# Chunked modulation with k-wise latents, conv units joined into the query stage, and a new split of the first up units, in a one-core layer kernel on Trainium2

## The reference, cut to what matters

```python
mod_lat = silu(c) @ w_ada + b_ada              # 6 * 1024 values; the context takes silu(c_ctx)
h  = rmsnorm(x, norm1_g)   * (1 + sc1)  + sh1  # the first two of six groups
hc = rmsnorm(ctx, norm1_g) * (1 + csc1) + csh1
p  = h @ w_in                                  # [kv latent 256 | rope key 32 | q latent 384 | conv x, B, C 3 * 512 | gates]
pc = hc @ w_in[:, :288]
q  = rmsnorm(q latent, q_norm_g)  @ w_uq       # 8 heads of 64 + 32 rotary
k, v = rmsnorm(kv latent, kv_norm_g) @ w_ukv   # 768 keys
o  = softmax(q k^T / sqrt(96)) v               # heads 8, queries 512
y_conv = (b_gate * dwconv3(c_gate * x_in)) @ w_conv_out
x = x + g1 * ((sigmoid(ga) * (o @ w_attn_out) + sigmoid(gc) * y_conv) @ w_o)
x = x + g2 * (silu(gate) * val) @ w_down       # gate, val = split(dwconv3(modulated rmsnorm(x) @ w_up))
out = rmsnorm(x, final_g)
```

## Time and profile before

| | |
|---|---|
| median of three runs | 853.37 us (852.27 to 854.98) |
| the profiled execution | 852.57 us |
| its span, first to last instruction | 850.8 us |
| mean granted TensorE clock | 0.983 |
| PE busy | 808.2 us, 3900 matmuls |
| DVE, ACT, POOL busy | 471.8, 373.9, 376.0 us |
| moved by DMA | 97.79 MB |

### The profile page before, as it was taken

The page is one execution under the profiler, slowest core; times in us unless marked ns, Lnnn a source line. Parts: engine busy times, 40 slices in busy tenths (PEclk is TensorE's granted clock), DMA queues, the critical chain, the costliest instruction groups (busy, mean ns, idle before and its releaser), DMA issues.

```text
span 850.8 us, 11214 instructions
## 1 busy us (share of the span) xinstructions
PE 808.2 (95%) x3900; PEld 672.6 (79%) x3900; DVE 471.8 (55%) x600; ACT 373.9 (44%) x571; POOL 376.0 (44%) x191
## 2 busy tenths in 40 slices
PE   6779978999999999999999989999999999999996
PEld 4458856888888888888788978888888888888884
DVE  5854698788887467788413646555555555100005
ACT  7763365656565442232234644444444444211124
POOL 0086274345533455455455034444444444444434
PEclk9979999999999999999999989999999999999998
DMA  9822211111111488777355014333333332323312
GB/s 317 289 74 61 64 50 50 50 50 29 48 50 26 153 252 259 252 247 219 127 198 148 2 50 123 99 99 99 99 99 98 92 96 93 96 95 98 99 50 99
DMA packets 119134, 97.79 MB, mean 115 GB/s; under 512 B 13532, under 2 KB 100857, under 8 KB 119097
## 3 DMA queue, kind: packets, MB, share of 16 engines
q1 hardware_dynamic: 119065, 97.28, 37.1%
q10 hardware_dynamic: 32, 0.01, 0.0%
HBM read 95.17 MB, written 2.10 MB: 114 GB/s over the span
## 4 chain that ended last, share of the span: by engine, by line
PE 59%; issue 16%; POOL 9%; DVE 6%; DMA 4%; ACT 2%; SPq 2%; POOLq 0%; DVEq 0%; ACTq 0%
PE ps L374 16%; PE ps L375 15%; PE ps L376 15%; POOL wlo L318 8%; PE ps L1444 7%; PE ps L1426 3%; PE ps L1415 2%; DMA raw<-w_in_dram 2%; DMA raw<-w_o_dram 1%; POOL ht L525 1%; DMA xt<-ctx_dram 1%; DMA xt<-x_dram 1%; DVE wlo L318 1%; DVE work L1022 1%; SPq L425 1%
## 5 line engine op out<-in xcount | busy, mean ns | idle before, releaser
L318 POOL TENSOR_TENSOR wlo<-raw,whi 128x1024 fp32r<-128x1024 f32 (+4 forms) x126 | 287.8, 2292 | 423.8 <-ACT whi L310 401.6
L374 PE MATMUL ps<-hhi,whi 128*128 128x512 f32 (+1 forms) x560 | 214.7, 383 | 8.8 <-DVE hlo L962 5.3
L375 PE MATMUL ps<-hlo,whi 128*128 128x512 f32 (+1 forms) x560 | 213.5, 381 | 0.0
L376 PE MATMUL ps<-hhi,wlo 128*128 128x512 f32 (+1 forms) x560 | 213.2, 381 | 0.0
L310 ACT ACTIVATE whi<-raw 128x1024 fp32r<-128x1024 f32 (+3 forms) x127 | 123.3, 980 | 141.1 <-PE ps L376 77.8
L374 PEld LDWEIGHTS ps<-hhi,whi 128*128 128x128 f32 x560 | 106.8, 191 | 30.1 <-issue 6.4
L376 PEld LDWEIGHTS ps<-hhi,wlo 128*128 128x128 f32 x560 | 106.7, 191 | 20.0
L375 PEld LDWEIGHTS ps<-hlo,whi 128*128 128x128 f32 x560 | 106.8, 191 | 19.6 <-issue 0.2
L1208 DVE SCALAR_TENSOR_TENSOR work<-ps,prm,work 128x511 f32<-128x511 f32 x44 | 33.0, 750 | 82.0 <-ACT work L875 81.1
L1113 DVE SCALAR_TENSOR_TENSOR adacc<-ada,cvec,adacc 128x1024 f32<-128x1024 f32 x28 | 64.9, 2357 | 14.8 <-DMA ada<-w_ada_dram 14.8
L875 ACT ACTIVATE work<-ps,prm 128x512 f32<-128x512 f32 x44 | 34.2, 778 | 79.2 <-PE ps L376 79.2
(11 more groups left out here) (245 smaller groups left out, 1430.1 us busy)
## 6 DMA issues: line engine op xcount, KB each, us to landing
raw<-w_up_dram SPq DMA_DIRECT2D x88, 256.0 KB, 3.1
raw<-w_in_dram SPq DMA_DIRECT2D x66, 256.0 KB, 3.4
ada<-w_ada_dram SPq DMA_DIRECT2D x32, 512.0 KB, 6.1
raw<-w_down_dram SPq DMA_DIRECT2D x44, 256.0 KB, 2.7
adaraw<-w_ada_dram SPq DMA_DIRECT2D x32, 256.0 KB, 4.8
raw<-w_o_dram SPq DMA_DIRECT2D x16, 256.0 KB, 3.0
xt<-x_dram SPq DMA_DIRECT2D x4, 512.0 KB, 6.4
raw<-w_attn_out_dram SPq DMA_DIRECT2D x8, 256.0 KB, 2.9
```

Of the source, the lines that this page charges most:

```text
L318: ins = (engine or nc.gpsimd).tensor_tensor(out=l, in0=r, in1=h.bitcast(F32), op=ALU.subtract)
L374: pe.matmul(o, l[0], r[0], start=start, stop=False)
L375: pe.matmul(o, l[0], r[1], start=False, stop=False)
L376: return pe.matmul(o, l[1], r[0], start=False, stop=stop)
```

## The change

- The first two groups of the modulation (shift and scale) are made in four chunks of 256 columns. The first chunk's columns come directly by fp32 products of the unsplit weights with the two conditioning vectors as two moving columns (`first_mods`); the other chunks go through the split, are summed as rows (`mod_sums`) and turned into columns by a product with a 4 x 2 selection matrix `sel` that also adds the high and low parts (`mod_columns`).
- The latents are no longer computed unit by unit over all k, but k by k: one row block of `w_in` with the 640 latent columns at a time (`latents`, five banks at once), as soon as the tile k of `h` is there. The kv weights stay in SBUF (`lkhi`, `lklo`) and the context is computed with them later, beside the rotary key, whose unit is cut in two.
- DVE makes the modulated value (`stream_value`) that POOL made; POOL splits the latent weights (`latent_lo`).
- The two context token tiles come in later, into the buffers of the first tokens.
- The kv norm's root and reciprocal are taken on 6 columns (`k_rms`, `k_inv`) and spread by six products with the identity.
- The first two units of the first conv tile are computed between the query heads, in pieces of 8, the third unit in the first two groups of attention, in pieces of 12; the other three conv tiles follow in pieces of 8, 8, 8, 8, 8, 8, 6, 6, 6, 6 (`CONV_TURNS`). The conv steps of ACT and DVE move accordingly.
- The maximum of a group is written to a spare PSUM column of the scores' second bank (`top`) and no longer to SBUF.
- The second halves of the first four up units: two units together over all k, then one, then one, where there were four together.

```diff
 U_ADA = 0
-U_Q = U_ADA + 2 * DT
-U_KV = U_Q + QT
-U_KR = U_KV + KVT
-U_UQ = U_KR + 1
-U_V = U_UQ + HEADS // 2
+U_KR = U_ADA + 2 * DT - 4
+U_UQ = (U_KR + 2, U_KR + 3, U_KR + 5, U_KR + 6)
+U_CX0, U_CC0 = U_KR + 4, U_KR + 7
+U_V = U_KR + 8
...
-CONV_PIECES = ((0, 8), (0, 8), (0, 8), (1, 8), (1, 8), (1, 8), (2, 12), (2, 12))
+CONV_TURNS = ((0, 2, 0, 12), (0, 2, 12, 12)) + tuple(
+    (j, n, at, size) for j in range(1, CT) for n, size in ((0, 8), (1, 8), (2, 6)) for at in range(0, 3 * DT, size))
...
+            def ada_load(u):
+
+                if u < 0:
+                    at = 0
+                else:
+                    at = (u // 4 + 1) * CHUNK
+                    if u < SLOTS:
+                        sp.wait_ge(s("ada0_used"), u + 1)
+                    else:
+                        sp.wait_ge(w_lo, u - SLOTS + 1)
...
+            for c_ in range(CHUNKS):
+                latent_load(2 * c_)
+                latent_load(2 * c_ + 1)
+                if c_ in (1, 2):
+                    token_load(TT + c_ - 1)
+                if c_ + 1 < CHUNKS:
+                    for u in range(4 * c_, 4 * c_ + 4):
+                        ada_load(u)
...
+            for c_ in range(1, CHUNKS):
+                for u in range(4 * c_ - 4, 4 * c_):
+                    ada_hi(u)
+                mod_rows1(c_)
+                for k in (2 * c_, 2 * c_ + 1):
+                    latent_hi(k)
+                    stream_hi(k)
+                if c_ > 1:
+                    upper_copy(TT + c_ - 2)
+                if c_ < 3:
+                    token_rms(TT + c_ - 1)
...
+            def first_mods(n):
+
+                pe.wait_ge(ada_loaded[n], 32)
+                for i in range(2):
+                    for m in range(4):
+                        at = i * T + m * P
+                        last = pe.matmul(ps[:, 3, 2 * m:2 * m + 2], adaraw[:, n, at:at + P], cvec[:, 2 * n + i, :],
+                                         start=(n, i, m) == (0, 0, 0), stop=(n, i, m) == (3, 1, 3))
+                last.then_inc(s("ada0_used"), 1)
...
+            for c_ in range(CHUNKS):
+                latents(2 * c_, every)
+                if c_ == 0:
+                    latents(1, (0, 1, 2))
+                if c_ + 1 < CHUNKS:
+                    for u in range(4 * c_, 4 * c_ + 4):
+                        mod_sums(u)
+                    latents(2 * c_ + 1, (0,) if c_ else (3,))
+                    mod_columns(c_ + 1)
+                    latents(2 * c_ + 1, (1, 2, 3, 4) if c_ else (4,))
+                else:
+                    latents(2 * c_ + 1, every)
+                if c_ in (1, 2):
+                    token_columns(TT + c_ - 1)
...
+                if h == 1:
+                    pe.wait_ge(s("p_raw"), KVT)
+                    latent_sums()
+                if 1 <= h < 4:
+                    conv_piece(0, 0, 8 * (h - 1), 8)
+                if h == 2:
+                    spread_inverse()
+                if h >= 5:
+                    conv_piece(0, 1, 8 * (h - 5), 8)
...
-                nc.vector.reduce_max(neg_max(g), wide(2 * (turn(g) % 2)), AX.X, negate=True).then_inc(s("nmax"), 1)
+                top = ps[:, 2 * (turn(g) % 2) + 1, C:C + 1]
+                nc.vector.reduce_max(top, wide(2 * (turn(g) % 2)), AX.X, negate=True).then_inc(s("nmax"), 1)
...
-            for i in range(DT):
-                pe.wait_ge(s("h2_lo"), DT + i + 1)
-                for m in range(4):
-                    last = up_half(m, 1, i)
-                    if i == DT - 1:
-                        last.then_inc(w_used, 1)
+            for ms in ((0, 1), (2,), (3,)):
+                for i in range(DT):
+                    pe.wait_ge(s("h2_lo"), DT + i + 1)
+                    for m in ms:
+                        last = up_half(m, 1, i)
+                        if i == DT - 1:
+                            last.then_inc(w_used, 1)
```

More of the change, by code:

```diff
@@ L442, in _, with token_load @@
-            for m in range(4):
-                slot = (U_UQ + m) % SLOTS
-                view = raw[:, slot % RAW, 0:2 * QT * QK].rearrange("p (k h n) -> p k h n", k=QT, n=QK)
-                load(sp, U_UQ + m, slot, [(view[:, :, h, :], rows_of(w_uq, 0, QT, (2 * m + h) * QK, QK)) for h in (0, 1)])
+            def token_load(t):
+                wait(sp, s("xT_ps"), t - TT + 1)
+                rows = x[t * P:(t + 1) * P, :] if t < TT else ctx[(t - TT) * P:(t - TT + 1) * P, :]
+                sp.dma_start(xt[:, t % TT, :], rows).then_inc(s(f"x_loaded{t}"), 16)
@@ new lines, in latent_load @@
+            def latent_load(k):
+                wait(sp, s("win_lo"), k - RAW + 1)
+                for to, at, n in ((0, 0, KVR), (KVR, KR_END, QR)):
+                    sp.dma_start(raw[:, k % RAW, to:to + n], w_in[k * P:(k + 1) * P, at:at + n]).then_inc(win_loaded[k % RAW], 16)
+            token_load(0)
+            ada_load(0 - SLOTS)
+            token_load(1)
+            for n in small_loads[0:3]:
+                rows_to(*n)
+            ada_load(1 - SLOTS)
+            for n in small_loads[3:6]:
+                rows_to(*n)
@@ L947, in _ @@
+            token_norm(3)
             dve.wait_ge(s("prm"), 1)
[L948 to L953 removed]
@@ L1269, in _, with mod_sums @@
+            def mod_sums(u):
+                c_, n = u // 4 + 1, u % 4
                 unit(u)
-                for b in range(2):
+                if n == 0:
+                    wait(pe, s("rows1"), c_ - 1)
+                    pe.wait_ge(s("mods1"), 4 * c_)
+                for i in range(2):
                     for w in (whi, wlo):
-                        last = pe.matmul(ps[:, 2 * half + b, :], chl[:, k, :], tile_of(w, u % SLOTS, b, 512),
-                                         start=k == 0 and w is whi, stop=k == DT - 1 and w is wlo)
+                        last = pe.matmul(ps[:, 3, :], chl[:, 2 * n + i, :], tile_of(w, u % SLOTS, i, T),
+                                         start=n == 0 and i == 0 and w is whi, stop=n == 3 and i == 1 and w is wlo)
@@ new lines, in mod_columns, with latents @@
+            def mod_columns(c_):
+                pe.wait_ge(s("rows1"), c_)
+                for m in range(4):
+                    last = pe.matmul(ps[:, 3, 2 * m:2 * m + 2], rows1[:, m * P:(m + 1) * P], sel[:], start=True, stop=True)
+                last.then_inc(s("cols1_ps"), 1)
+            def latents(k, tiles):
+                pe.wait_ge(s("win_lo"), k + 1)
+                pe.wait_ge(s("h_lo"), k + 1)
+                for m in tiles:
+                    w = (tuple(t[:, k % 3, m * P:(m + 1) * P] for t in (lqhi, lqlo)) if m < QT else
+                         tuple(t[:, k, (m - QT) * P:(m - QT + 1) * P] for t in (lkhi, lklo)))
+                    last = mm3(pe, ps[:, LATENT_BANK[m], :], w, (hhi[:, k, :], hlo[:, k, :]), k == 0, k == DT - 1)
+                    if k == DT - 1:
+                        last.then_inc(s("lat_ps"), 1)
+                    elif m == QT + KVT - 1:
+                        last.then_inc(s("win_used"), 1)
@@ new lines, in latent_sums, with spread_inverse @@
+            def latent_sums():
+                pe.wait_ge(s("q_sum"), QT - 1)
+                for t in range(TT):
+                    pe.matmul(ps[:, 6, t:t + 1], work[:, 3, t * P:(t + 1) * P], ones[:, 0:1], start=True, stop=True)
+                pe.wait_ge(s("k_ssq"), 1)
+                for t in range(KT):
+                    last = pe.matmul(ps[:, 6, 8 + t:9 + t], sqk[0][:, t * P:(t + 1) * P], ones[:, 0:1], start=True, stop=True)
+                last.then_inc(s("stat_ps"), 1)
+            def spread_inverse():
+                pe.wait_ge(s("k_rinv"), 1)
+                for t in range(KT):
+                    last = pe.matmul(ps[:, 4 + t // TT, t % TT * P:(t % TT + 1) * P], k_inv[:, t:t + 1].to_broadcast([P, P]), ident[:],
+                                     start=True, stop=True)
+                last.then_inc(s("k_spread"), 1)
@@ new lines, in conv_piece @@
+            def conv_piece(j, n, at, count):
+                u = conv_unit(j, n)
+                if at == 0:
+                    unit(u)
+                    if n > 0:
+                        pe.wait_ge(s("c_x" if n == 1 else "c_prod"), j + 1)
+                    elif j > 0:
+                        pe.wait_ge(s("c_z"), j)
+                for i in range(at, at + count):
+                    k, term = i // 3, i % 3
+                    last = pe.matmul(ps[:, 7, :], tile_of(wlo if term == 2 else whi, u % SLOTS, k),
+                                     (hlo if term == 1 else hhi)[:, k, :], start=i == 0, stop=i == 3 * DT - 1)
+                if at + count == 3 * DT:
+                    last.then_inc(w_used, 1)
```

648 lines of the change are left out of this document (369 added, 279 removed).

## The result

| | before | after |
|---|---|---|
| median | 853.35 us (6 runs, 851.70 to 854.98) | 847.04 us (6 runs, 845.82 to 849.58) |
| profiled execution, its span | 852.57, 850.8 | 847.1, 845.3 |
| PE busy, granted clock | 808.2, 0.983 | 820.0, 0.993 |

The ratio after to before is 0.9921, 95% interval 0.9899 to 0.9942: 6.7 us faster, give or take 1.8. The forecast was 842, in a range of 831 to 852.

What follows compares the result with a forecast made beforehand. It took TensorE (PE) to bound the kernel nearly everywhere, and loads the start. Terms -18.3 + 16.4 + 7.9 - 11.0 - 6.3 = -11.3 gave 841.3 us for the profiled execution, 842 against the median, range 831 to 852.

Steps and rivals of the forecast that it cites:

- start: Up to the first latent matmul: it comes at 30.2 us instead of 48.47, with products at the slow pace, -18.3.
- latents and modulation in chunks: First latent matmul to query start: 49.5 us becomes 65.9, of which 59.8 is work and the rest waits and locks, +16.4.
- query stage: Query start to first score matmul: 34.9 us becomes 42.8, with 48 conv matmuls coming in, +7.9.
- attention: First score matmul to last matmul of attention, 155.8 us before: 48 fewer conv matmuls, -11.0.
- up units: First up units: -3.2 us for the hole before the second group, -3.1 for the half clock behind it, -6.3.
- Rival (a): The start runs at full clock, first latents near 20 us, total 833 us; chance 0.17.
- rival (d): Slower: the loads pace the modulation chunks, at half the rate +19.5 us, total 861; chance 0.06.
- DMA over 0.9 busy: Sign that the forecast is wrong: DMA busy above this share in the modulation chunks.
- (e): All POOL locks against VectorE's splits in the chunks stay uncovered, +8.6 us, total 850; chance 0.10.
- I leave the waits at 4.9: In attention, PE's waits stay at 4.9 us, VectorE's saving of some 11 us paying for the shorter groups.
- rival (b): Attention is paced by its maximum, exp, normalize, transpose loop; fewer conv matmuls give nothing, +11.0 us, total 853; chance 0.12.
- From there to the end PE ran through; nothing later eats it: Behind the up units' hole: the -6.3 us gain is kept to the end, no later stage takes any back.

Runs made afterwards that it cites:

- e9_max_sbuf: The changed kernel with the maximum of a group written to SBUF again instead of a PSUM column; 852.21 us, ratio 0.9979 to the kernel before.
- e3: The kernel before with only the up edit, second halves of the first four up units as two, one, one; 848.77 us, ratio 0.9928.
- e4: The changed kernel with the second halves of the first four up units four together again; 852.71 us, ratio 0.9975 to the kernel before.
- e5_pad256: The changed kernel with 192 unused bytes behind `small`, putting later tiles 256 bytes further than in the kernel before; 844.38 us, ratio 0.9868 to the kernel before.

## Why the prediction was right, and where it was wrong

The range held the time, and faster was right. The sum was 5 us too large a gain. Term by term, forecast against the profiled execution:

| term | forecast | measured |
|---|---|---|
| start | -18.3 | -16.8 |
| latents and modulation in chunks | +16.4 | +16.8 |
| query stage | +7.9 | +9.1 |
| attention | -11.0 | -12.7 |
| up units | -6.3 | -6.4 |
| all behind attention that isn't touched | 0 | +4.4 |

**Start.** The slow pace was the right choice. A group of products took 3.41 where I took 3.4, and the first began at 6.71 (6.8). The last group ended at 25.97 + 3.41 = 29.4, 1.2 after my 28.2: the wait for VectorE's copies of the parameters was 1.51 and not 0.8, a token's transposes 1.74 from start to next start and not 1.6. The chain on VectorE and ScalarE behind took 2.3; I had 2.0, though the 0.7, 0.4 and 0.7 that I wrote down add to 1.8. The granted clock column says 1.00 in these stretches, and also from 31.6 to 38.0, where 512-column matmuls lie 0.43 apart; at the start the pace tells the clock, not the column. Rival (a) is out. The page I cited (the Trainium skill, TensorE: Matmul & The Clock Gate, "Part 4: PE-mode transpose") speaks of transposes alone; eight of them took 1.74 us here, the slow pace, which agrees. The column products stood among them, and no run shows what they would do alone at the start.

**Chunks.** Nearly the sum, by luck: errors cancel. I had 3.8 us of waits of the sums in chunks 2 and 3; there was one, 0.76. The wait of chunk 1 was 1.64 for 1.3, but I priced it as a wait only: a half clock followed it in this execution (0.50 from 48.2 to 50.0, six matmuls, 1.2 us), on top of the twelve slow ones at the start, which I had. 168 matmuls at the worse distance are 1.1, by count. 59.8 of work as I had it, 2.4 of waits, 1.2 and 1.1 make 64.5 of the 66.3; the rest is not placed. The sign that I had named for rival (d), DMA over 0.9 busy, did come: 0.94 from 51 to 61. But the rate there was 290 GB/s and not half, PE was busy for all 10 us, and its waits in this stage are for VectorE. So (d) is out, and the sign was badly chosen. VectorE's `hlo` subtractions took 951 ns in the mean against the 690 of the first, some 2 us over eight, which I put down to POOL's splits beside them without a run that shows it; PE's waits leave no room for 9.6, so (e) is out.

**Query stage.** 1.2 us too short. The waits were 0.76 for a conv unit and 0.85 for the value tile at 139.03, together 1.6 for my 1.7: the first was forecast (0.8), the second was not, and the 0.9 behind `CX0` did not come. So the matmuls were short-priced: about 0.7 is the distance, by count, the rest is not placed. In the five executions with a half clock near 104 it took 45.4 to 45.6.

**Attention.** The step "I leave the waits at 4.9" failed, on the good side. Matmuls are 150.9 - 11.0 = 139.9, so waits were 3.2. With the maximum in SBUF they would have been 7.0 (e9_max_sbuf). Taking 48 matmuls out gives 155.8 to 146.9, -8.9, with the maximum in SBUF, and 154.5 to 143.1, -11.4, with it in PSUM. The first is rival (b) in part: its loop of maximum and exp eats 2.1 of the 11.0. (My words for it, that the 19.3 were all of VectorE's slack there, were wrong: it was busy 120.3 of the 145 us, so idle 24.7.) The second is the full 11.0, and the 1.3 that the maximum is worth by itself makes the -12.7. These are differences of single executions. The one-column product is slow with both operands in SBUF, 0.552 and 0.596 us, and 0.158 with one in PSUM. By the Trainium skill, SBUF - State Buffer, "Who interferes with whom", a VectorE instruction with two SBUF inputs contends with GpSimd's reads; that agrees with these means.

**Up units.** Right in both parts, 3.4 and 3.0 for 3.2 and 3.1, and alone (e3) as in the change (e4).

**The step that failed** is the last sentence of that paragraph, "From there to the end PE ran through; nothing later eats it", and its silent twin for the stages between. PE did run through; each matmul became dearer. I had priced the declarations of new tiles at nothing, not even naming them. Down +3.4, projection +0.6, "to columns" +0.9 are measured; about 1.1 and 0.7 within the chunks and the query stage are counts of matmuls times 0.0067: 6.7 us, more than the whole distance of 5.8 between forecast and the profiled execution. e5_pad256 returns 4.5 of it.

## What to carry to other kernels

When a stage that a change does not touch gets slower without a wait, compare the distance of two starts, not busy shares, and then the addresses of its two operands; in a kernel like this keep stationary and moving operands a multiple of 256 bytes apart, and pad where small tiles are declared in front of large ones. Price a wait on PE with what the clock does behind it: one of 3.2 us cost 6.2 (e3). Look for an edit's gain in what it lets another edit give: the maximum in PSUM was worth 1.3 us alone and 3.8 beside the shorter groups.
